# A gated MoE step: half of the down product in three fp32r terms, with its operands split per block

## What is computed

```python
def one_group(args):
    xg, e = args          # 128 gathered rows of one expert
    return (jax.nn.silu(xg @ w_gate[e]) * (xg @ w_up[e])) @ w_down[e]
```

## Time and profile before

| | us |
|---|---|
| median of three runs | 2063.76 (2061.64 to 2064.91) |
| profiled execution, whole | 2062.67 |
| its span, first to last instruction | 2061.0 |
| granted TensorE clock, mean over the span | 0.962 of full speed |

### The profile page before, as it was taken

One profiled execution on the slowest core, in us unless ns is written; L12 is line 12 of the kernel. 1 busy time (PEld: TensorE's weight loads), 2 busy tenths in 40 slices (PEclk: granted clock), 3 DMA queues, 4 the chain that ended last, 5 costly groups with the idle time before them and its releaser, 6 DMA issues.

```text
span 2061.0 us, 29206 instructions
## 1 busy us (share of the span) xinstructions
PE 1922.1 (93%) x9115; PEld 1444.6 (70%) x9116; DVE 1087.0 (53%) x1900; ACT 754.2 (37%) x1322; POOL 328.6 (16%) x337
## 2 busy tenths in 40 slices
PE   6999999999689999998999999993899999999966
PEld 2778777887467777775888888872577777666622
DVE  4577777777420000005355555556566666666657
ACT  3355544454220101014111111112466666666622
POOL 0011001110000000001011111111133443333311
PEclk8999999999799999999999999996899999999988
DMA  9122222222475445537534344428587554879686
GB/s 373 62 94 104 103 104 79 84 99 93 150 277 205 163 173 189 205 116 279 187 143 143 143 143 143 143 72 279 178 305 266 191 176 172 296 278 356 239 302 286
DMA packets 185731, 380.84 MB, mean 185 GB/s; under 512 B 43144, under 2 KB 113976, under 8 KB 178492
## 3 DMA queue, kind: packets, MB, share of 16 engines
q1 hardware_dynamic: 147084, 319.36, 43.1%
q0 software_dynamic: 20848, 52.32, 6.7%
q10 hardware_dynamic: 17760, 8.67, 1.4%
HBM read 295.42 MB, written 104.26 MB: 194 GB/s over the span
## 4 chain that ended last, share of the span: by engine, by line
PE 63%; DMA 4%; DVE 2%; SPq 2%; issue 1%; ACT 0%; ACTq 0%; POOL 0%; DVEq 0%; POOLq 0%
PE fin L152 16%; PE fin L154 16%; PE fin L153 16%; PE fin L2200 8%; PE fin L2169 2%; PE fin L1629 1%; PE fin L1656 1%; DMA w_gate_raw<-in_w_in 1%; DMA mixer_parts<-oT_split 1%; DMA gathered<-weighted_rows 1%; PE fin L2240 1%; PE fin L1204 1%; DMA pb_b<-out_b_projected 1%; PE fin L2188 1%; DVE expert_gate_up L2145 0%
## 5 line engine op out<-in xcount | busy, mean ns | idle before, releaser
L2097 DVE TENSOR_TENSOR gate_up_lo<-expert_gate_up,gate_up_hi 128x2048 fp32r<-128x2048 f32 x102 | 233.6, 2292 | 147.5 <-ACT gate_up_hi L2002 147.5
L2002 ACT CAST gate_up_hi<-expert_gate_up 128x2048 fp32r x102 | 194.3, 1907 | 82.3 <-issue 78.1
L152 PE MATMUL mix<-w_mix_hi,hT_hi 128*128 128x512 f32 (+3 forms) x544 | 203.3, 374 | 6.2 <-DVE hT_lo L593 4.9
L1147 DVE SCALAR_TENSOR_TENSOR ma_rows<-tanh_rows,fin 128x512 f32<-128x512 f32 (+1 forms) x34 | 21.8, 683 | 338.1 <-PE fin L154 187.7
L153 PE MATMUL mix<-w_mix_hi,hT_lo 128*128 128x512 f32 (+3 forms) x544 | 199.0, 366 | 0.0
L154 PE MATMUL mix<-w_mix_lo,hT_hi 128*128 128x512 f32 (+3 forms) x544 | 198.4, 365 | 0.0
L2200 PE MATMUL fin<-expert_down,hidden_T 128*128 x400 | 182.0, 598 | 5.2 <-ACT hidden_T L2010 4.2
L152 PE MATMUL fin<-gate_up_hi,gathered_T_hi 128*128 128x512 f32 x400 | 161.7, 404 | 4.2 <-DVE gathered_T_lo L2088 4.2
L154 PE MATMUL fin<-gate_up_lo,gathered_T_hi 128*128 128x512 f32 x400 | 157.7, 394 | 0.0
L153 PE MATMUL fin<-gate_up_hi,gathered_T_lo 128*128 128x512 f32 x400 | 157.4, 393 | 0.0
L1932 POOL DMA_INDIRECT gathered<-h_rows,row_tokens x52 | 131.0, 2520 | 46.8 <-issue 28.8
(11 more groups left out here) (319 smaller groups left out, 3809.8 us busy)
## 6 DMA issues: line engine op xcount, KB each, us to landing
expert_gate_up<-in_w_gate SPq DMA_DIRECT2D x32, 1024.0 KB, 7.9
expert_gate_up<-in_w_up SPq DMA_DIRECT2D x32, 1024.0 KB, 10.9
expert_down<-in_w_down SPq DMA_DIRECT2D x32, 1024.0 KB, 12.1
h_parts<-hT_split SPq DMA_DIRECT2D x16, 1024.0 KB, 5.1
mixer_parts<-oT_split SPq DMA_DIRECT2D x32, 512.0 KB, 8.3
w_ada_part<-in_w_ada SPq DMA_DIRECT2D x16, 1024.0 KB, 10.7
h_parts_b<-hT_split SPq DMA_DIRECT2D x16, 1024.0 KB, 4.8
expert_down<-weighted_rows SPq DMA_DIRECT2D x12, 1024.0 KB, 8.4
```

The costliest lines, as they stand in the source:

```text
L152: nc_mm(out, left[0], right[0], start=first, stop=False)
L1147: last = nc.vector.scalar_tensor_tensor(out=ma[0:m, par, at], in0=tg[0:m, at], scalar=1.0, in1=ps[2 + n][0:m, :], op0=ALU.add, op1=ALU.mult)
L2002: nc.scalar.copy(wg[par][0][:, n * HG:(n + 1) * HG], ring[:, bass.ds(slot * GU + n * HG, HG)]).then_inc(w_hi, 1)
L2097: nc.vector.tensor_tensor(wg[par][1][:, at], ring[:, bass.ds(slot * GU + n * HG, HG)], wg[par][0][:, at].bitcast(F32), ALU.subtract).then_ ...
```

## The change

In the down product, the first half of the contraction is made in three fp32r terms, the second half stays in fp32. For that the first halves of both operands are split for each block: the down weights on ScalarE (`down_high`, after `weigh`) and VectorE (`down_low`, between the halves of `weights`); hidden on ScalarE (`hidden`, now two copies of 128 columns, the first into fp32r) and VectorE (`hidden_low`, last in the step). The split down weights `wd` and the turned hidden `hT` have one buffer each, so ScalarE waits for the down product of the block before. `silu_e` is gone (silu is written over the tanh), and tanh and hidden have one buffer in place of two. TensorE's down product now waits for VectorE's low parts.

```diff
     def on_scalar(act):
...
         def hidden(b, par):
             act.wait_ge(h_turned, b + 1)
-            nc.scalar.activation(hT[par][:, :, :], ps[4][:, 0:2 * P].rearrange("p (k m) -> p k m", m=P), ACT.Copy, scale=0.5).then_inc(hT_ready, 1)
+            if not isinstance(b, int) or b > 0:
+                act.wait_ge(down, b)
+            nc.scalar.activation(hT[0][:, :], ps[4][:, 0:P], ACT.Copy, scale=0.5)
+            nc.scalar.activation(hT_rest[:, :], ps[4][:, P:2 * P], ACT.Copy, scale=0.5).then_inc(hT_ready, 1)
+
+        def down_high(b):
+            need, slot = listed(act, 1, b), listed(act, 0, b)
+            act.wait_ge(d_ready, need)
+            if not isinstance(b, int) or b > 0:
+                act.wait_ge(down, b)
+            nc.scalar.copy(wd[0][:, :], downs[:, bass.ds(slot * DOWN, D)]).then_inc(d_hi, 1)
...
             weights(b + 2, par, (0,))
             weigh(b - 1, (slot - 1) % 4, landed, before)
+            down_high(b)
             weights(b + 2, par, (1,))
             records(b + 1, (slot + 1) % 4)
             hidden(b, par)
...
     def on_vector(dve):
...
+        def down_low(b):
+            slot = listed(dve, 0, b)
+            dve.wait_ge(d_hi, b + 1)
+            nc.vector.tensor_tensor(wd[1][:, :], downs[:, bass.ds(slot * DOWN, D)], wd[0][:, :].bitcast(F32), ALU.subtract).then_inc(d_lo, 1)
+
+        def hidden_low(b):
+            dve.wait_ge(hT_ready, b + 1)
+            nc.vector.scalar_tensor_tensor(out=hT[1][:, :], in0=ps[4][:, 0:P], scalar=0.5, in1=hT[0][:, :].bitcast(F32),
+                                           op0=ALU.mult, op1=ALU.subtract).then_inc(hT_lo, 1)
 
         def step(b, par):
             silu(b, par)
             turned(b + 1, 1 - par)
-            weights(b + 2, par)
+            weights(b + 2, par, (0,))
+            down_low(b)
+            weights(b + 2, par, (1,))
+            hidden_low(b)
...
         def out(b, par):
-            need, slot = listed(pe, 1, b), listed(pe, 0, b)
-            pe.wait_ge(d_ready, need)
-            pe.wait_ge(hT_ready, b + 1)
+            slot = listed(pe, 0, b)
+            pe.wait_ge(d_lo, b + 1)
+            pe.wait_ge(hT_lo, b + 1)
             if not isinstance(b, int) or b > 0:
                 pe.wait_ge(y_out, b)
             for n in range(2):
-                for k in range(2):
-                    at = slot * DOWN + k * D + n * 512
-                    last = nc.tensor.matmul(ps[5 + n][:, :], hT[par][:, k, :], downs[:, bass.ds(at, 512)], start=(k == 0), stop=(k == 1))
+                at = slice(n * 512, (n + 1) * 512)
+                three(nc.tensor, ps[5 + n][:, :], (hT[0][:, :], hT[1][:, :]), (wd[0][:, at], wd[1][:, at]), True, False)
+                last = nc.tensor.matmul(ps[5 + n][:, :], hT_rest[:, :], downs[:, bass.ds(slot * DOWN + D + n * 512, 512)], start=False, stop=True)
             last.then_inc(down, 1)
```

More of the change, by code:

```diff
@@ L1789, in experts @@
     wg = ready["split_weights"]
[L1790 to L1793, removed]
+    th = sb("tanh_e", [P, EH])
+    h = sb("hidden", [P, EH])
+    hT = [sb(f"hidden_T_{part}", [P, P], F32R) for part in ("hi", "lo")]
+    hT_rest = sb("hidden_T_rest", [P, P])
+    wd = [sb(f"down_{part}", [P, D], F32R) for part in ("hi", "lo")]
     y = sb("y_block", [P, 2, D])
@@ L1802, in experts @@
     gu, tanhed, silued, h_ready, h_turned, hT_ready = [sem(f"e_{n}") for n in ("gate_up", "tanh", "silu", "h", "h_turned", "hT")]
+    d_hi, d_lo, hT_lo = sem("e_down_hi"), sem("e_down_lo"), sem("e_hT_lo")
     down, y_out, stored = sem("e_down"), sem("e_y_out"), (sem("e_stored0"), sem("e_stored1"))
@@ L2005, in silu @@
             act.wait_ge(gu, b + 1)
-            nc.scalar.activation(th[:, par, :], ps[2 + par][:, 0:EH], ACT.Tanh, scale=0.5).then_inc(tanhed, 1)
+            nc.scalar.activation(th[:, :], ps[2 + par][:, 0:EH], ACT.Tanh, scale=0.5).then_inc(tanhed, 1)
         def hidden(b, par):
             act.wait_ge(h_turned, b + 1)
-            nc.scalar.activation(hT[par][:, :, :], ps[4][:, 0:2 * P].rearrange("p (k m) -> p k m", m=P), ACT.Copy, scale=0.5).then_inc(hT_ready, 1)
+            if not isinstance(b, int) or b > 0:
[8 more added lines that the diff above has]
+            nc.scalar.copy(wd[0][:, :], downs[:, bass.ds(slot * DOWN, D)]).then_inc(d_hi, 1)
         def weigh(b, slot, landed, before):
@@ L2035, in on_scalar @@
         weights(2, 0)
+        down_high(0)
         hidden(0, 0)
@@ L2090, in turned, with weights @@
             last.then_inc(xT_lo, 1)
-        def weights(b, par):
+        def weights(b, par, parts=(0, 1)):
             slot = listed(dve, 0, b)
-            for n in range(2):
+            for n in parts:
                 at = slice(n * HG, (n + 1) * HG)
@@ L2101, in silu @@
             dve.wait_ge(tanhed, b + 1)
-            nc.vector.scalar_tensor_tensor(out=sg[:, par, :], in0=th[:, par, :], scalar=1.0, in1=ps[2 + par][:, 0:EH],
+            nc.vector.scalar_tensor_tensor(out=th[:, :], in0=th[:, :], scalar=1.0, in1=ps[2 + par][:, 0:EH],
                                            op0=ALU.add, op1=ALU.mult).then_inc(silued, 1)
             dve.wait_ge(silued, b + 1)
-            nc.vector.tensor_tensor(h[:, par, :], ps[2 + par][:, EH:2 * EH], sg[:, par, :], ALU.mult).then_inc(h_ready, 1)
+            nc.vector.tensor_tensor(h[:, :], ps[2 + par][:, EH:2 * EH], th[:, :], ALU.mult).then_inc(h_ready, 1)
+        def down_low(b):
[6 more added lines that the diff above has]
+                                           op0=ALU.mult, op1=ALU.subtract).then_inc(hT_lo, 1)
         def step(b, par):
@@ L2120, in on_vector @@
         weights(2, 0)
+        down_low(0)
+        hidden_low(0)
         total = listed(dve, TOTAL, 0)
@@ L2185, in turn_h @@
             if not isinstance(b, int) or b > 0:
-                pe.wait_ge(hT_ready, b)
+                pe.wait_ge(hT_lo, b)
             for k in range(2):
-                last = nc.tensor.transpose(ps[4][:, k * P:(k + 1) * P], h[:, par, k * P:(k + 1) * P], ident[:, :])
+                last = nc.tensor.transpose(ps[4][:, k * P:(k + 1) * P], h[:, k * P:(k + 1) * P], ident[:, :])
             last.then_inc(h_turned, 1)
         def out(b, par):
-            need, slot = listed(pe, 1, b), listed(pe, 0, b)
-            pe.wait_ge(d_ready, need)
-            pe.wait_ge(hT_ready, b + 1)
+            slot = listed(pe, 0, b)
+            pe.wait_ge(d_lo, b + 1)
+            pe.wait_ge(hT_lo, b + 1)
             if not isinstance(b, int) or b > 0:
```

## The result

The changed kernel takes 2090.22 us (median of 4, 2089.66 to 2090.62), the kernel before 2063.61 (median of 4, 2061.64 to 2064.91). The ratio is 1.0133, 95% interval 1.0118 to 1.0148: the change makes the kernel 1.3% slower. Forecast were 2091 and 2073 to 2107.

The account below looks back on a forecast made before the run. TensorE bounds the loop before at 10.04 us a period; the new wait makes it 10.55, so 48 periods add 24.3 and the end 3.0, +27.3 on 2062.67, forecast 2091, range 2073 to 2107.

Parts of the forecast that it names:

- tanh to the down product of the same block: Expert loop: ScalarE and VectorE steps up to the low hidden and its release, summing to T + 12.04.
- down product to the tanh after it: Expert loop: from down product of b to T(b+2), 9.33 in the kernel before, less 0.35: 8.98.
- The new wait: Down product waits for low hidden, queued on VectorE behind the second half of gate and up weights; 1.7 late.
- the halving: Expert loop: the chain from tanh through the down product spans two periods, 21.02, so one period is 10.51.
- The price of products by their spacing: TensorE: fp32 product 0.86, fp32r 0.228 each by spacing; three terms for one save 0.35 us a block.
- The alternation: Expert loop: long and short periods in turn, as the chain joins every second block; 0.04 added, giving 10.55.
- the buffer's loop: Split down weights' single buffer: down product, list reads, high part and VectorE's low parts, 10.37, below 10.51 but near.
- Rival B: Expert loop: the down weights' buffer decides if list reads take 2.0 instead of 1.55; period 10.82, 2104; chance 0.17.
- the first chain: Expert loop: tanh to down product, 12.04, then on to the tanh after it, 8.98; two periods, 21.02.
- Rival A: Expert loop: TensorE stays the bound and the three terms' saving comes through, 17.6 us, giving 2046; chance 0.07.
- Rival C: Expert loop: repeated holes lower the clock for every down product, +1.5 a period, 2163; chance 0.03.
- The end: After the last tanh: the last down product starts 3.4 later and lasts some 0.4 less, +3.0.

Follow-up runs that it names:

- e7: Changed kernel with hidden ahead of the second half of the gate and up weights, and ScalarE's list reads ahead of its waits: 2044.98 us, ratio 0.9921.
- e8: Kernel before, with only the list reads for row tokens and gate and up weights made early: 2060.48 us, ratio 0.9986.
- e1: Changed kernel with hidden's copies and low part ahead of the second half of the gate and up weights: 2063.63 us, ratio 1.0004.
- e3: Changed kernel without VectorE's low part of hidden; the high part stands in for it, so the product is wrong: 2056.64 us.
- e12: Changed kernel with an added 128x512 ScalarE copy ahead of the high down part, and the down weights' list reads ahead of the wait: 2102.06 us.
- e10: Changed kernel with only the two list reads for the down weights moved ahead of `weigh`: 2088.55 us, period 10.55.
- e9: Changed kernel with the list reads for row tokens and gate and up weights moved to the start of the step: 2084.44 us, period 10.43.
- e4: Changed kernel with one fp32 product in place of the three terms on TensorE, all splits and waits kept: 2105.55 us, period 10.87.
- e6: Changed kernel with one more 128x512 ScalarE copy ahead of the high part of the down weights: 2110.72 us, period 10.94.
- e5: Kernel before with single tanh, hidden and turned hidden buffers and silu written over the tanh, nothing split: 2062.45 us, ratio 1.0001.

## Why the prediction was right

Forecast 2091, measured 2090.2. By the steps of the sum (the first two measured ones are means over the blocks of the loop; in the block shown above they are 1702.33 to 1714.34 = 12.01 and 1703.88 to 1712.97 = 9.09):

| step | predicted | measured |
|---|---|---|
| tanh to the down product of the same block | 12.04 | 12.04 |
| down product to the tanh after it | 8.98 | 9.08 |
| period | 10.51, with 0.04 for alternation 10.55 | 10.55 |
| the loop, 48 periods | +24.3 | +24.3 |
| after the last tanh | +3.0 | +2.45 |
| ahead of block 1's tanh | 0 | +0.45 |
| what the terms save TensorE | 0.35 a block | 0.33 (e7 against e8) |

*The new wait* was placed and sized as it came out. e1 and e3 show it by taking its two ingredients away, the place in the order and the instruction, and e12 shows the halving: its chain from the tanh to the down product is 0.51 longer (12.55) and its period 0.26. The changed kernel's period is 0.87 over e7's 9.68, where TensorE never waits; the prediction had 0.86 of standing still. (The idle time in the view is less, 0.64 on average, since the records of matmuls reach into the hole.) In the 12.04 small errors cancel: the first cast starts 3.44 after the tanh and not 3.52, the high part 1.18 after `weigh` and not 1.15, and the product 0.38 after the start of the low hidden and not 0.35.

*The price of products by their spacing* held: by the spacing the saving was to be 0.35, and 0.33 came out of it. An estimate from the sentence in the Trainium skill's "FP8 and Floating Point Precision", section TensorE Precision Notes, on four passes for fp32, with an fp32r product taken as one pass, would have had it at 0.46. What was 0.10 too low is the step from the down product to the tanh. Its first term starts at 1703.88 and its second at 1704.19, 0.31 later and not 0.23; e7 has the same 0.31 without a hole. Halved, this makes the period 0.05 longer than the sum has it, (12.04 + 9.08) / 2 = 10.56.

*The alternation* is there: holes of about 0.5 and 0.75 in turn. But the 0.04 that was added for it isn't. In e10 the buffer's loop is shorter, and while many of its periods swing wider (1683.47, 1694.29 and 1704.65 are successive tanhs, 10.82 and 10.36), their mean is 10.55 as in the changed kernel. So the 10.55 of the sum is luck in its last digits: 0.05 too little in the step from the down product to the tanh, and 0.04 too much for the alternation, about 2 us each over the loop.

*Rival B*, the buffer's loop, exists, and its size was nearly right. I had it at 10.37; e9, where it is the bound, has a period of 10.43 (10.50 in the rows shown). The small differences are the way from the down product to the high part, 3.25 + 1.55 = 4.80 by my sum and 4.84 on average in e9's trace, and the end, 0.35 by my sum from the start of the low hidden to the down product and 0.39 in the trace. It thus stands 0.12 below the chain from the tanh, where my sum had 0.14, and in the changed kernel it decides nothing. In e4 and e6, whose times I had worked out from the first chain, it matters: it is about half of the miss of 9 us in e4, and all of that of 8 us in e6.

*Rival A*, TensorE remaining the bound, is what e7 makes true: 2045, where the rival had named 2046. Its condition had been put at a chain 1.7 shorter. The Trainium skill's "Perfetto Trace Analysis" has, under Identifying the Most-Contended Engine, the engine of highest occupancy optimised first, and judges TensorE's headroom by its weight loads and not by its matmuls' busy time. Here that engine was TensorE by either figure (93%, weight loads 70%, VectorE 53%). Its busy time in the loop fell by 5.2 us (481.10 to 475.91), and the kernel got slower, until the order of the other two engines was mended. *Rival C*, a falling clock, didn't occur: the granted clock stayed 1.00 with a hole in nearly every period.

*The end*: the last down product starts 12.14 after its tanh (1976.87 to 1989.01), 3.5 later than before, as said. The product takes 5.19 and not 5.39, so 0.2 came back there and not 0.4: up to 1992.6 us its granted clock was 0.50, the lower of the two levels, and 1.00 from 1993.0 on (0.62 over these 5.19 us; before, after 4.16 idle in place of 6.91, it was 0.68 over the 5.39). The remaining 0.8 lies behind it, which I had not looked at. From the last tanh to the end the kernel before takes 108.9 us, e5 109.2 and e8 110.2, with the same work there, so 0.8 is within what differs from run to run.

## What to carry to other kernels

An engine that bounds a loop is relieved only if the operands of its cheaper form arrive in time, so work out when the last new operand is ready in its engine's written order, not how busy that engine is. A small instruction on which the bounding engine waits belongs ahead of large ones that prepare for later; and a register read between a wait and the instruction that needs it belongs ahead of the wait. When two loops stand within a few per cent of each other, shortening one shows little or nothing: test both together, and price a disturbance by the loop that it lengthens most.

## What the runs showed of the hardware

Reading two entries of a list in SBUF into registers held ScalarE for 1.45 us between the DMA that precedes and the cast that follows (1703.97 + 0.35 to 1705.77 in the changed kernel). In e7, where the reads come earlier, the first cast follows the turned rows without idle time, 1.83 after the tanh; the reads cost nothing visible where they are now.

GpSimd's gather of rows, off the path in all kernels, is recorded at a median of 2665 ns in the kernel before and of 1015 in the changed one, with the same data. Its instruction and place in GpSimd's order are the same; the rest of the period around it moved. Kernel before and changed kernel, 1500 to 1900 (ns min/median/max):

```profile
L1932 POOL DMA_INDIRECT gathered<-h_rows,row_tokens x40: 1888/2665/2777, 1499.1 to 1890.8; - x40
L1934 POOL DMA_INDIRECT gathered<-h_rows,row_tokens x38: 1012/1015/2843, 1499.9 to 1890.9; - x38
```

The traces of all fourteen kernels, 1475 to 1930, tell when it is long. They hold 620 gathers. 320 start while VectorE has more than 0.15 us left of a subtraction that makes a low part of the weights (128x2048 or 128x1024, both inputs in SBUF), and each of them ends 0.88 to 0.90 us after that subtraction ends, whether 0.2 or 2 us of it were left. The other 300 take 1.01 to 1.03 us, without exception. So the gather stands still until VectorE's instruction is done. What the two share isn't seen in a trace, and no run was made for this alone.
